# Softmax of three attentions rewritten around a Newton step, and wide projections that end in four quarters with their normalisation taken along

## The reference

```python
def block(args):                       # differential attention, 128 queries
    sc = jnp.einsum('bqhcd,bkhcd->bhcqk', qb, k).astype(jnp.float32) * scale
    p = masked_softmax(sc, chunk_mask(blk, s)[None, None, None])
    a = p[:, :, 0] - lam * p[:, :, 1]
    return jnp.einsum('bhqk,bkhe->bqhe', a.astype(v.dtype), v)
o = rms_norm(o, subln_g) * (1.0 - lambda_init)

# latent attention: the same with one map and p @ v; grouped attention:
probs = jax.nn.softmax(jnp.concatenate([logits + bias, sink_logit], -1), -1)[..., :-1]

def rms_norm(x, g):
    y = xf * lax.rsqrt(jnp.mean(xf * xf, axis=-1, keepdims=True) + NORM_EPS)
    return y * g
```

## Time and profile before

| | us |
|---|---|
| median of 3 runs | 2879.71 (2878.49 to 2882.27) |
| the profiled execution | 2881.92 |
| its span, first to last instruction | 2880.1 |
| mean granted TensorE clock | 0.953 |

### The profile page before, as it was taken

How to read it: one execution, slowest core, us unless ns; L and a number is a source line. 1 busy time by engine, 2 the same in 40 slices (tenths; PEclk the granted TensorE clock), 3 DMA queues, 4 the chain that set the end, 5 groups by cost and what they waited for, 6 DMA issues and landing times.

```text
span 2880.1 us, 47150 instructions
## 1 busy us (share of the span) xinstructions
PE 2621.7 (91%) x16067; PEld 2359.9 (82%) x16067; DVE 1870.8 (65%) x3168; ACT 1288.6 (45%) x1907; POOL 718.0 (25%) x738
## 2 busy tenths in 40 slices
PE   7659997799898988999999999778978999999998
PEld 6549976689797977899999998668977899999997
DVE  5877845768554999555555555585998555555554
ACT  4345543556444236444444444354155444444443
POOL 0000000000000010255555555010200355555554
PEclk9779998899999999999999999979999999999999
DMA  6124552146645321666666665404412666666664
GB/s 197 34 81 148 181 163 70 52 140 183 196 140 160 126 74 39 196 186 186 184 186 187 185 184 180 146 23 139 140 51 80 185 188 184 188 185 187 183 188 131
DMA packets 167707, 421.46 MB, mean 146 GB/s; under 512 B 13648, under 2 KB 64397, under 8 KB 167358
## 3 DMA queue, kind: packets, MB, share of 16 engines
q1 hardware_dynamic: 162894, 412.82, 47.0%
q10 hardware_dynamic: 4720, 7.37, 0.8%
HBM read 419.06 MB, written 1.08 MB: 146 GB/s over the span
## 4 chain that ended last, share of the span: by engine, by line
PE 75%; DVE 19%; ACT 3%; issue 2%; DVEq 1%; SPq 0%; ACTq 0%; DMA 0%; POOL 0%
PE PS L422 24%; PE PS L423 24%; PE PS L424 24%; DVE arena L1356 4%; DVE oh L1747 3%; DVE oh L1744 1%; PE PS L522 1%; DVE lo L1237 1%; DVE arena L1710 1%; ACT arena L882 1%; DVE arena L1714 1%; DVEq L1747 1%; DVE arena L1644 1%; DVE arena L1648 1%; DVE arena L1645 1%
## 5 line engine op out<-in xcount | busy, mean ns | idle before, releaser
L1237 DVE TENSOR_TENSOR lo<-raw,hi 128x1024 fp32r<-128x1024 f32 x732 | 1008.0, 1380 | 806.4 <-ACT hi L851 804.6
L851 ACT ACTIVATE hi<-raw 128x1024 fp32r<-128x1024 f32 x732 | 766.4, 1054 | 516.2 <-PE PS L424 508.1
L422 PE MATMUL PS<-xh,hi 128*128 128x256 f32 x2784 | 789.6, 284 | 0.0
L423 PE MATMUL PS<-xl,hi 128*128 128x256 f32 x2784 | 789.2, 283 | 0.0
L424 PE MATMUL PS<-xh,lo 128*128 128x256 f32 x2784 | 789.1, 283 | 0.0
L422 PEld LDWEIGHTS PS<-xh,hi 128*128 128x128 f32 x2784 | 535.7, 192 | 8.8
L423 PEld LDWEIGHTS PS<-xl,hi 128*128 128x128 f32 x2784 | 535.5, 192 | 8.0
L424 PEld LDWEIGHTS PS<-xh,lo 128*128 128x128 f32 x2784 | 535.1, 192 | 0.0
L422 PE MATMUL PS<-hi,Ah 128*128 128x512 f32 x1024 | 405.0, 396 | 8.2 <-DVE lo L1237 7.1
L424 PE MATMUL PS<-hi,Al 128*128 128x512 f32 x1024 | 405.3, 396 | 0.0
L423 PE MATMUL PS<-lo,Ah 128*128 128x512 f32 x1024 | 405.0, 396 | 0.0
(11 more groups left out here) (212 smaller groups left out, 3074.1 us busy)
## 6 DMA issues: line engine op xcount, KB each, us to landing
raw<-in_peer_u SPq DMA_DIRECT2D x256, 512.0 KB, 3.6
raw<-in_peer_v SPq DMA_DIRECT2D x256, 512.0 KB, 4.3
raw<-in_ffn_w_up SPq DMA_DIRECT2D x88, 512.0 KB, 3.6
raw<-in_ffn_w_down SPq DMA_DIRECT2D x44, 512.0 KB, 3.8
raw<-in_peer_w_q SPq DMA_DIRECT2D x32, 512.0 KB, 3.8
raw<-in_da_w_qkv SPq DMA_DIRECT2D x24, 512.0 KB, 4.3
raw<-in_conv_w_in SPq DMA_DIRECT2D x24, 512.0 KB, 3.6
raw<-in_attn_w_qkv SPq DMA_DIRECT2D x12, 512.0 KB, 4.3
```

The source lines that it names most:

```text
L422: pe.matmul(o, ah, bh, start=start, stop=False)
L423: pe.matmul(o, ah, bl, start=False, stop=False)
L851: cp.activation(hi[:, s, 0:size], raw[:, s, 0:size], ACT.Copy).then_inc(hi_made, 1)
L1237: V.tensor_tensor(lo[:, s, 0:size], raw[:, s, 0:size], hi[:, s, 0:size].bitcast(F32), ALU.subtract).then_inc(lo_made, 1)
```

## The change

**Attentions.** The mask or bias is no longer added by PE. DVE does scores plus mask or bias, negated, and the minimum of it along the row in one instruction (`tensor_tensor_reduce`), from PSUM into SBUF, once per tile; its accumulator is read by an instruction of its own. GQA's bias is stored key-reversed for it, so its keys and values are reversed by matmuls with an anti-diagonal matrix, and the bias table is read by four DMAs instead of two. The reciprocal goes: ACT makes exp(-2u) as a guess, POOL adds 1 to it, ACT makes tanh as before, and two DVE instructions (`begin`, `finish`) make a Newton step on 1/(1 - tanh). POOL also doubles the shift of each map (`double`). The square moves behind the transpose, where ACT reads PSUM anyway. Row sums are made by PE: each values matmul is followed by one with the same weights and a column of ones. In the differential attention the two maps are no longer combined before the values: each is transposed and multiplied by itself, DVE divides and subtracts the results (`head_out`), ACT squares them head by head. Transposes of queries and keys are spread over the steps. The auxiliary banks are three (5 to 7, in turn), since bank 4 (and 3) holds the row sums.

**Wide projections and norms.** The last two blocks are taken quarter by quarter (t, h). DVE adds each quarter as it is done, ACT squares it; mean, root and scale of tile 0 come before the fourth quarter is squared; tile 1 follows. Each tile is scaled half by ACT, half by DVE, and PE transposes tile 0 while tile 1 is made. The sqrt table is loaded by a dummy before the first quarter. f0 and f1 scale and multiply by the gain in one instruction, f1's output leaves in three DMAs. Two blocks ahead are split before the adds, not three. The bias table DMAs are issued behind norm n6 and not before it.

```diff
 def scores(s):                                                     # PE
     qt, kt, c2 = a.place(s)
-    b = aux((nm, "s", s), [(at, 2 * s + 2)])
+    b = aux((nm, "s", s), [(am, 2 * s + 2)], bank())
     ...
     for t, c, n in a.segs:
-        pe.matmul(PS[:, b, c:c + n], ..., start=True, stop=False)
-        if a is gqa:
-            i = pe.matmul(PS[:, b, c:c + n], anti, gbias[:, t, s, :], start=False, stop=True)
-        else:
-            i = pe.matmul(PS[:, b, c + n - P:c + n], ident, mask, start=False, stop=True)
+        i = pe.matmul(PS[:, b, c:c + n], ..., start=True, stop=True)
+def values(s):                                                     # PE
+    ...
+        for n, kt in ks:
+            w = a.PT[:, s % a.ring, n * P:(n + 1) * P]
+            pe.matmul(o, w, a.v(kt, h), ...)
+            i = pe.matmul(PS[:, den_bank(a, h), 2 * s + t:2 * s + t + 1], w, ones, ...)
+for s in range(a.nsub + 5):                                        # PE
+    for j in new_pairs(a, s) if s < a.nsub else ():
+        pair(j)
+    if s < a.nsub:
+        scores(s)
+    if 0 <= s - 3 < a.nsub:
+        turn_weights(s - 3)
+    ...
+    if s >= 5:
+        values(s - 5)
+def soft(s):                                                       # ACT
+    for t, c, w in a.segs:
+        cp.activation(a.hb[...], a.S[:, s, c:c + w], ACT.Exp, scale=-2.0, bias=twice[:, s, t:t + 1])
+    act.wait_ge(S(f"{nm}_guess_made"), 2 * s + 2)
+    for t, c, w in a.segs:
+        cp.activation(a.S[:, s, c:c + w], a.S[:, s, c:c + w], ACT.Tanh, scale=-1.0, bias=nmax[:, s, t:t + 1])
+def probs(s):                                                      # ACT
+    cp.activation(a.PT[:, s % a.ring, 0:w_all], PS[:, aux_bank[(nm, "p", s)], 0:w_all], ACT.Square,
+                  scale=0.5, bias=minus1)
-        V.reciprocal(e, e).then_inc(S(f"{nm}_recip_made"), 1)      # DVE
+    if 0 <= s - 2 < a.nsub:                                        # DVE, each step
+        begin(s - 2)
+    if s < a.nsub:
+        largest(s)
+    if 0 <= s - 2 < a.nsub:
+        finish(s - 2)
+    if a is da and s % 2 == 1 and s >= 7:
+        head_out((s - 7) // 2)
+    V.scalar_tensor_tensor(e, e, -1.0, a.hb[...], ALU.add, ALU.mult)   # begin
+    V.scalar_tensor_tensor(e, e, 4.0, a.hb[...], ALU.add, ALU.mult)    # finish
+    V.tensor_tensor_reduce(a.S[:, s, c:c + w], PS[:, b, c:c + w], extra, -1.0,
+                           neg_sinks[:, s:s + 1] if a is gqa else 3.0e38, ALU.add, ALU.min,
+                           nmax[:, s, t:t + 1])                        # largest, per tile
-    e = a.S[:, s, 0:cols]                                          # POOL
-    nc.gpsimd.tensor_scalar(e, e, -1.0, 1.0, ALU.mult, ALU.add)
+    double(s + 1)
+    plus_one(s)
 def wide(name, ah, al, kcs):                                       # PE
-    for kc in range(kcs):
+    for kc in range(kcs - 2):
     ...
+    for t in range(TT):
+        for h in range(2):
+            for kc in (kcs - 2, kcs - 1):
+                i = part(kc, t, h)
+            if not (t and h):
+                i.then_inc(part_summed, 1)
 def add_x(name, B_end, then, gain):                                # DVE
+    for q, (t, w) in enumerate(quarters):
+        if q < 3:
+            dve.wait_ge(part_summed, 3 * list(xadds).index(name) + q + 1)
+        else:
+            mean(then, 0)
+            if "peer" not in name:
+                root(then, 0)
+            dve.wait_ge(split_used, B_end)
+        V.tensor_tensor(X[:, t, w], X[:, t, w], PS[...], ALU.add).then_inc(x_new, 1)
```

More of the change, by code:

```diff
@@ new lines, in attention @@
+                if a is gqa:
+                    b = aux((nm, "v"), [(S("v_turned"), 1)], bank())
+                    for t in range(TT):
+                        i = pe.matmul(PS[:, b, t * T:(t + 1) * T], anti,
+                                      gqkv[:, t, (GQA_H + GQA_KV) * GQA_DH:(GQA_H + 2 * GQA_KV) * GQA_DH], start=True, stop=True)
+                    i.then_inc(aux_full, 1)
+                for s in range(a.nsub + 5):
+                    for j in new_pairs(a, s) if s < a.nsub else ():
+                        pair(j)
@@ L1316, in rope, with wide @@
+                if "peer" in name:
+                    root(then, 0)
+                scaled(then, 0)
+                mean(then, 1)
+                root(then, 1)
+                scaled(then, 1)
+                if gain is not None:
+                    turned(then, gain)
+            def wide(name, n, then, gain):
+                splits_to(plan[name][0] + n + 2)
+                add_x(name, plan[name][0] + n, then, gain)
             def rope(x1, x2, cos, sin, t1, t2, o1=None, o2=None):
```

535 lines of the change are left out of this document (286 added, 249 removed).

## The result

The changed kernel takes 2849.1 us (median of 4, 2846.8 to 2850.0) beside 2880.2 us for the one before (4 runs, 2878.5 to 2882.3): a ratio of 0.9887, 95% interval 0.9875 to 0.9900. It is faster by 31 us, where the prediction said 70; 2849 lies outside its range of 2786 to 2838. The profiled execution took 2849.97 us, with a span of 2848.2.

A forecast was written before the change was run, and what follows sets the result against it. It took DVE's share, over half attention reciprocals, and the norms' gaps as winnable, expecting the bank loop to decide afterwards. 2881.9 - 41 (attentions) - 28.9 (norms) = 2812, median 2810; forecast 2797 to 2823, range 2786 to 2838.

The forecast's parts named there:

- DVE's prices: Attentions, per map: two products 0.93 us and two minima with accumulator reads 0.9, so 1.85 for 3.07.
- Rival (c): Attentions: fused minimum goes at the reciprocal's pace, 2.5 us for 0.6; 71 us more, 2881, no change; chance 0.03.
- POOL's doubling with handoffs 0.3: Latent attention's bank loop: GpSimd's doubling with its handoffs takes 0.3 us of the 3.65 from last score matmul to transposes.
- Rival (b): Attentions: handoffs, accumulator reads or POOL cost 0.5 us a step more; 24 us, 2834; chance 0.20 together with (d).
- (d): Norms: quarters don't overlap as DVE's splits and ACT's squares meet; norms gain 9, 2830; chance 0.20 together with Rival (b).
- rival (e): Attentions: TensorE stays at its lower clock; 99 us more, 2909; sign is a clock under 0.7 in an attention; chance 0.04.
- the attentions' ends: Before and after the steps: first minimum at 4.8 us (was 12) and a tail of 14.2 in the latent attention.
- PE's pitch: Attentions on PE: 0.11 us for each instruction up to 128 columns, a ones column included; row sums 0.66 a map.
- The bank loop: Latent attention: transposes wait for ACT's square of an earlier map; 3.65 + 2.8 = 6.45 us for two steps.
- rival (a): Attentions: the bank loop doesn't close and engines' own work is last, latent step 2.75; 15 us more gain, 2795; chance 0.17.
- Norms: Gaps from PE's last matmul to the next projection close to about 6.5 us; 28.9 us gained in all.
- n6: Norm before the grouped projection: four table DMAs take 5.4 us, PE waits 4.3; some 14 become 11.7, gain 2.3.

The follow-up runs named there:

- c4: Changed kernel with GpSimd's addition in two operations, doubling on VectorE, 64 ones columns, table DMAs two and two, reordered start, latent square first: 2783.1 us.
- e1: Changed kernel with GpSimd's addition of one written as two operations (times 1.0, plus 1.0): 2830.8 us.
- e2: Changed kernel with the doubling of the negated maxima moved from GpSimd to VectorE, behind the minima: 2804.9 us.
- e4: Changed kernel with each row sum matmul of the attentions streaming 64 columns of ones instead of one: 2827.7 us.
- e3: Changed kernel with ACT squaring map s-3 ahead of the exponential and tanh of map s, in the latent attention alone: 2838.5 us.
- e6: Changed kernel with two of the four bias table DMAs issued only behind ACT's first copy of the grouped projection: 2840.6 us.
- e9: Changed kernel with VectorE's second product of a map waiting until GpSimd's doubling of the same step is done: 2839.1 us.

## Why the prediction was off, step by step

**DVE's prices: right.** Products 560 and 553 ns for 557, minimum 419 and 481 for 476, an accumulator read 83 for 70 to 190. Rival (c), a minimum at the reciprocal's pace, is out. With GpSimd out of the way a differential head takes 6.04, 6.57 and 6.05 us in c4, for the predicted 6.3, and that attention 65.1 for 67.

**"POOL's doubling with handoffs 0.3": the first step that failed.** It is one term in the loop, with no row behind it and no bounds, and it was priced as if GpSimd worked alone. With its handoffs it took 0.58 us, 0.475 of it itself, since DVE's product holds it up. The addition of one was not priced at all: its line looked the same as before, but it had lost its second operation, and 511 ns became 1168. In the differential attention the chain of a step became doubling, addition, product, 7.28 us a head for 6.3, at full clock; e1 takes that to 6.63 and e2 to 6.2. By its pace at full clock this step explains some 8 of the 30 us by which the attentions were missed (an estimate: 4.5 heads of 1.0, 15 latent steps of 0.07 and 7.5 pairs of grouped steps of 0.4, 7.50 for 7.1). Rival (b), handoffs or POOL 0.5 us a step more, named the place and gave 2834; it had 0.20 together with (d). That it came nearest of all is luck in part: its 24 us are more than GpSimd's own share, and it had no term for the clock.

**The clock: the second step that failed, and by these estimates the larger.** Every step of the sum was priced at full clock, though 118 of the 250 us of before had run at 1.2 GHz, and rival (e) was held down to 0.04 with the argument that a busier PE has the higher clock. It is false here: the clock fell behind 6.83 us in which PE was busy for 5.64, and stayed down for 20.48 in which it was never idle. The prediction's own sign of (e), a clock under 0.7 in an attention, came true in the grouped one (0.69), and (e)'s prices were right: a grouped step at 1.2 GHz takes 6.29 and 5.97 us in turn for 6.1 in the changed kernel, a latent one 5.20 for 5.2 in e1. What was wrong is the share of the time at 1.2 GHz, which is neither none nor all: 123 of 239 us. What is left of the 30 us, some 22, is this and whatever is wrong in the attentions' ends, which no run separates. The grouped attention, predicted at 75 us, took 90.4. e4 changes nothing but the width of the sums and gets 75.3, so the clock was worth 15 us there and 24.2 in all three. The two failures feed each other: e2, which shortens the chain on other engines, also brings the clock to 0.89. It has 18.5 us less than e4, of which the pace at full clock explains some 11 and the clock the rest, since e4 still has some 53 us at 1.2 GHz for 43. How the whole difference to the forecast divides between the two can't be told further, since they don't add up: 15.2, 42.7 and 24.2 us alone, 48.3 together.

**PE's pitch: right.** At full clock the four instructions of a values matmul and its sum take 0.44 us with one column and 0.45 with 64, 0.11 each, as the earlier trace rows had it. What was missing is that the width, though it costs no time by itself, goes with the clock of the whole stretch.

**The bank loop: right in size, wrong as the last bound.** Two latent steps took 6.55 us for the predicted 6.45: 2.90 on PE for 2.8, and 3.65 for 3.65 from the last score matmul to the transposes. That the second is exact is luck: the doubling with its handoffs is 0.28 too small in it, the minimum 0.18 too large (0.82 for 1.0), and the overlap between ACT's instructions makes up the rest. The waits ahead of the transposes, 0.31 and 0.44 in turn, are 0.75 in two steps for 0.85; the wait of about 0.8 ahead of every transpose in the prediction's last part took the wait of two steps for that of one. e3 breaks the loop and gains 3 to 5 us. In c4 a latent step takes 2.71 us, which is rival (a)'s 2.75.

**Norms: better than forecast but for one.** n1, n2, n3 and n7 close in 5.93 us for 6.5, f0 with n4 in 11.70 for 12.5, f1 in 8.15 for 10.0; the seven besides n6 gain 31 us for 26.6. At n1 the last half scale was put at 4.3 behind PE's end and came at 3.7; the step from there to the projection, 2.2, took 2.27.

**n6: a term with a linear price that wasn't linear.** Four DMAs were put at twice the 2.72 us of two; they took 13. The stall is 9.52 us for 4.3, and n6 lost 2.5 where it should have gained 2.3, though its projection started 6.35 us behind PE's end for 7.4. e6 shows the cause, and that waiting is all it takes.

**The start: missed.** The order of the transposes at n0 was not costed, since no row of the sum touched it; it costs 1 to 2 us. Some 5 us more are spread over the projections behind the norms (191.15 us from n1 to n2 became 192.55, but 191.27 in c4). For these the clock is a likely cause (argued, not tested): over the first 5 us behind n1 it was 0.90 before, 0.66 in the changed kernel and 1.00 in c4, which by itself makes 1.2 us more than before and 1.7 more than c4 (an estimate), for the 1.40 and 1.28 measured. The other stretches are open.

**The sum.** Attentions 30 us too optimistic, n6 4.8 and the start 2.4, the spread 5, less 4.4 at the norms: 38, and 2810 becomes 2848.

## What to carry to other kernels

An engine that is idle for most of the program is not free inside a chain: price each of its instructions by a row of the same form, with the same number of operations and the same neighbour on DVE, and look at what its line looks like after the edit even where the step "stays". When a sum is moved onto TensorE as matmuls of one column, give them as many columns as cost nothing, and read the granted clock of the stretch in the kernel before: where part of it runs at the lower level, a sum at full clock alone is a bound and not a forecast. And a price for two DMAs in a queue says little about four.

## What the runs showed of the hardware

- GpSimd's tensor-scalar instruction took 1168 ns for 384 fp32 columns and 1488 for 512 with one operation (after), and 513 and 632 with two (e1).
- GpSimd's doubling, a tiny instruction, took 0.47 us beside DVE's product of 384 columns, 0.60 beside the one of 512 (after), and 222 ns beside none (e9); DVE's product took 0.78 us beside GpSimd's addition and 0.55 without.
- TensorE's clock fell to 1.2 GHz behind 6.83 us with PE busy for 5.64, and stayed there for 20.48 us in which PE was never idle (after); with 64 columns for one in the sum matmuls it stayed at 2.4 behind the same 6.83 us (e4), and over the grouped attention it was 0.89 for 0.69. What else moves it is open: four kernels with the same attentions had 0.68 to 0.77.
- The issue of a pair of DMAs of 512-byte rows held ACT's queue 2.25 us when nothing stood ahead of it, 10.65 behind another pair, and 2.93 with that pair 14 us ahead.
